# A squared-ReLU feed-forward computed by Strassen's seven block products

## The reference, cut to what matters

```python
x = x + mixed @ w_out[l]
h = _rms_norm(x, norm_mlp_g[l])
x = x + jnp.square(jax.nn.relu(h @ w_up[l])) @ w_down[l]
return _rms_norm(x, norm_final_g)
```

## Time and profile before

| | |
|---|---|
| median of 3 runs | 1752.92 us (1752.18 to 1753.65) |
| the profiled execution, its own time | 1755.03 us |
| its span, first to last instruction | 1752.9 us |
| TensorE clock granted, mean of the span | 0.986 |
| PE busy | 1672.7 us, 95% |
| DVE busy | 863.5 us, 49% |
| ACT busy | 683.2 us, 39% |
| POOL busy | 4.1 us |
| HBM read, written | 79.70 MB, 4.23 MB |

### The profile page before, as it was taken

How to read it: one execution, slowest core, us unless ns; L and a number is a source line. 1 busy time by engine, 2 the same in 40 slices (tenths; PEclk the granted TensorE clock), 3 DMA queues, 4 the chain that set the end, 5 groups by cost and what they waited for, 6 DMA issues and landing times.

```text
span 1752.9 us, 22515 instructions
## 1 busy us (share of the span) xinstructions
PE 1672.7 (95%) x8188; PEld 1373.6 (78%) x8188; DVE 863.5 (49%) x1738; ACT 683.2 (39%) x1484; POOL 4.1 (0%) x20
## 2 busy tenths in 40 slices
PE   6999898997999999999999999999999999999997
PEld 5777677774788887788888888888888888888886
DVE  5788888865566666422226344233333333323244
ACT  6467767773666666411114222121212121212121
POOL 0000000000000000000000000000000000000000
PEclk9999999997899999999999999999999999999998
DMA  5210100110020200112123302111111111111102
GB/s 180 78 33 25 37 25 25 37 37 0 13 61 14 60 13 22 34 43 57 42 71 106 109 25 72 49 48 48 48 48 48 48 48 48 48 48 48 36 12 96
DMA packets 126110, 84.95 MB, mean 48 GB/s; under 512 B 2888, under 2 KB 122696, under 8 KB 125904
## 3 DMA queue, kind: packets, MB, share of 16 engines
q1 hardware_dynamic: 126032, 83.94, 16.1%
HBM read 79.70 MB, written 4.23 MB: 48 GB/s over the span
## 4 chain that ended last, share of the span: by engine, by line
PE 78%; DVE 11%; issue 5%; ACT 5%; DMA 0%; ACTq 0%; DVEq 0%; SPq 0%
PE ps L525 36%; PE ps L829 20%; PE ps L569 11%; PE ps L638 3%; DVE work L1271 2%; PE ps L608 2%; PE ps L619 2%; DVE ps L1292 2%; PE ps L514 1%; ACT work L986 1%; DVE o_nat L1314 1%; ACT tmp L978 1%; DVE tmp L1256 1%; DVE work L1299 1%; DVE work L1263 1%
## 5 line engine op out<-in xcount | busy, mean ns | idle before, releaser
L569 PE MATMUL ps<-hspl,wsp 128*128 128x512 f32 x1536 | 427.6, 412 | 8.4 <-ACT tmp L942 6.6
L569 PEld LDWEIGHTS ps<-hspl,wsp 128*128 128x128 f32 x1536 | 268.9, 192 | 55.5 <-ACT tmp L942 8.6
L525 PE MATMUL ps<-hspl,wsp 128*128 128x512 f32 x1176 | 276.3, 392 | 0.6 <-ACT keep L1007 0.6
L525 PEld LDWEIGHTS ps<-hspl,wsp 128*128 128x128 f32 x1176 | 222.4, 189 | 47.1 <-issue 0.8
L829 PE MATMUL ps<-hspl,wsp 128*128 128x512 f32 x768 | 177.4, 390 | 0.0
L829 PE MATMUL ps<-hspl,work 128*128 128x512 f32 x768 | 175.4, 389 | 0.0
L1501 DVE TENSOR_TENSOR keep<-keep,ps 128x1024 f32<-128x1024 f32 x64 | 78.2, 1221 | 193.5 <-PE ps L829 192.5
L829 PEld LDWEIGHTS ps<-hspl,wsp 128*128 128x128 f32 x768 | 143.5, 188 | 32.6 <-DVE keep L1501 2.6
L829 PEld LDWEIGHTS ps<-hspl,work 128*128 128x128 f32 x768 | 144.2, 188 | 29.9
L525 PE MATMUL ps<-work,wsp 128*128 128x512 f32 x648 | 153.5, 390 | 0.0
L525 PEld LDWEIGHTS ps<-work,wsp 128*128 128x128 f32 x648 | 121.7, 188 | 25.7 <-issue 0.5
(11 more groups left out here) (158 smaller groups left out, 1738.9 us busy)
## 6 DMA issues: line engine op xcount, KB each, us to landing
raw<-in_w_in SPq DMA_DIRECT2D x47, 512.0 KB, 3.8
raw<-in_w_up SPq DMA_DIRECT2D x16, 512.0 KB, 4.0
tmp<-in_w_up SPq DMA_DIRECT2D x16, 512.0 KB, 4.0
raw<-in_w_down SPq DMA_DIRECT2D x16, 512.0 KB, 3.4
tmp<-in_w_down SPq DMA_DIRECT2D x16, 512.0 KB, 3.3
keep<-in_x SPq DMA_DIRECT2D x8, 512.0 KB, 6.6
fbias<-f_rows SPq DMA_DIRECT2D x8, 512.0 KB, 4.8
tmp<-in_x SPq DMA_DIRECT2D x8, 512.0 KB, 4.3
```

The lines of the kernel that those rows point to most:

```text
L525: ins = pe.matmul(ps[:, cols], w(wp, k), mv(mp, k)[:, cols], start=(k == 0 and n == 0), stop=(k == ks - 1 and n == 2))
L569: ins = pe.matmul(psp(u, g), wsp[:, c % 2, wp, k * P:(k + 1) * P], hspl[:, mp, k, cols], start=(n == 0), stop=(n == 23), skip_group_check= ...
```

## The change

The two feed-forward products are computed by the scheme of Strassen in Winograd's form. A product of two 2x2 block matrices takes 7 block products in place of 8, and in exchange sums of blocks before and after: with blocks a of the weights, blocks b of the activations, S1 = a21+a22, S2 = S1-a11, S3 = a11-a21, S4 = a12-S2, and likewise T1 to T4 of b.

Up and down become two stages. The up stage has 16 steps q, each a pair of 128 hidden columns; the blocks split the input channels and the tokens in halves. Each of its 7 products has 4 tiles x 3 = 12 matmuls. The down stage has 32 steps, 8 groups of hidden columns by 4 pairs of output channels, with 7 products of 2 tiles x 3 = 6 matmuls. The program is written out, without a loop.

The hidden values are stored in the DRAM tensor `hidden` as the seven forms that the down stage multiplies (`store_t`, `store_u11`, `store_u21`, `store_u22`), and loaded again (`load_b`). `kp` holds other values in the up stage, so the residual is stored in `x_mid` and loaded back (`reload`).

POOL forms the sums of weight blocks (`sums`, four 128-partition sums per step, 512 columns wide in the up stage and 256 in the down stage), of `h` (`h_sums`), of hidden values (`hidden_sums`, four sums 512 wide per up step), and adds three copied partial results to `kp` in the down stage (`add_s1`, `add_s2`, `add_s3`, 512 wide). ACT casts each of the seven forms (`form_hi`), DVE subtracts (`form_lo`). Partial sums stay in PSUM: ACT copies the bank (`copy_s1`, `copy_s2`, `copy_s3`) before the next product adds to it.

The output projection now goes over the two slots of `wsp` and in the order 0, 4, 1, 5, ..., and the forms of `h` are made beside it. After the down stage the sum of squares is kept by halves of the tokens.

The diff below is cut: declarations, the `t` and `u` stores that repeat a pattern, and the final stage's squares are left out.

```diff
+def block_products(n):
+    order = ((n, 0), (n - 1, 4), (n, 1), (n, 2), (n - 1, 5), (n, 3), (n - 1, 6))
...
+def block_forms(n):
+    order = [(n, j) for j in (4, 5, 6)] + [(n + 1, j) for j in (0, 1, 2, 3)]
...
+            def load_b(c, j):
+                if c < 2:
+                    sp.wait_ge(done, PRODUCT[UP - 1, j])
+                else:
+                    sp.wait_ge(done, PRODUCT[UP + 4 * (c - 2) + 3, j])
...
+                if n == UP - 1:
+                    load_b(0, 0)
+                    load_b(0, 1)
+                    load_b(0, 2)
+                    sp.wait_ge(a_lo, FORM[UP - 2, 5])
+                    reload(0)
+                    load_a_all(UP)
+                if n < UP:
+                    store_u11(n)
+                if n == UP - 1:
+                    sp.wait_ge(a_lo, FORM[UP - 2, 6])
+                    sp.wait_ge(a_sum, 4 * (UP - 1) + 3)
+                    reload(1)
+                    load_b(0, 3)
+                if 1 <= n < UP:
+                    store_u21(n - 1)
+                if n == UP:
+                    sp.wait_ge(a_lo, FORM[UP - 1, 6])
+                    reload(2)
+                    sp.wait_ge(t_ok, 4 * (UP - 1))
+                    sp.wait_ge(u11_out[0], 16 * (UP // 2))
+                    sp.wait_ge(u22_out[0], 16 * (UP // 2))
+                    reload(3)
+                    load_b(0, 4)
+                    load_a11(UP + 1)
+                    load_a12(UP + 1)
+                    load_a21(UP + 1)
+                    load_b(0, 5)
+                    load_a22(UP + 1)
+                    store_u21(UP - 1)
+                    load_b(0, 6)
+                    load_a_all(UP + 2)
...
+            def sums(q, ops):
+                pool.wait_ge(a_in[q % 4], 64 * (q // 4 + 1))
+                a = {x: a_raw_at(q, x) for x in FORM_RAW + ("a21",)}
+                for i in ops:
+                    if i == 1:
+                        if q >= 2:
+                            pool.wait_ge(done, PRODUCT[previous(q), 3])
...
+            def hidden_sums(q):
+                pool.tensor_tensor(t3b, u22[q % 2], u12, ALU.subtract).then_inc(t_ok, 1)
+                pool.tensor_tensor(t2b, t3b, u11[q % 2], ALU.add).then_inc(t_ok, 1)
+                pool.tensor_tensor(u12, u12, u11[q % 2], ALU.subtract).then_inc(t_ok, 1)
+                pool.tensor_tensor(t4b, u21, t2b, ALU.subtract).then_inc(t_ok, 1)
...
+            def add_s3(q):
+                c = down_c(q)["22"]
+                pool.wait_ge(s3_ok, q + 1)
+                pool.wait_ge(c22_ok, q + 1)
+                pool.tensor_tensor(c, c, s3[:], ALU.add).then_inc(add3, 1)
...
+            for n in range(1, NQ + 1):
+                if n >= 2 and n - 2 < UP:
+                    hidden_sums(n - 2)
+                if UP <= n < NQ:
+                    add_s1(n)
+                if UP <= n - 1:
+                    add_s3(n - 1)
+                if n + 1 < NQ:
+                    sums(n + 1, (1, 2, 3, 4))
+                if UP <= n < NQ:
+                    add_s2(n)
...
-            def mlp_block(b, first):
-                for j in range(4):
-                    if first:
-                        if j < 2:
-                            pe.wait_ge(resid, KC - 1 + j)
-                        else:
-                            pe.wait_ge(u_r, j - 1 + PRIME)
...
+            def product(q, j):
+                pe.wait_ge(a_lo, FORM[q, j])
+                if j == 0:
+                    if q < 3:
+                        pe.wait_ge(resid, 7 if q < 2 else 8)
+                        pe.wait_ge(c21_ok, q - 2)
+                elif j == 1:
+                    if q < 2:
+                        pe.wait_ge(xres, KC)
+                    else:
+                        pe.wait_ge(c11_ok, q - 1)
+                elif j == 2:
+                    pe.wait_ge(s1_ok, q + 1)
+                elif j == 3:
+                    if q == 0:
+                        pe.wait_ge(resid, KC)
+                    elif q < 3:
+                        pe.wait_ge(mean_out, 1)
+                    else:
+                        pe.wait_ge(c12_ok, q - 2)
+                elif j == 4:
+                    pe.wait_ge(s2_ok, q + 1)
+                elif j == 5:
+                    pe.wait_ge(s3_ok, q + 1)
+                else:
+                    pe.wait_ge(c22_ok, q + 1)
+                if q >= UP and (q - UP) % 4 == 0:
+                    pe.wait_ge(b_lo, HID_FORM[(q - UP) // 4, j])
+                o = bank_b(q) if j == 1 else bank_c(q) if j in (3, 6) else bank_a(q)
+                ks = 4 if q < UP else 2
+                for k in range(ks):
+                    if q == 0:
+                        h_form_ready(j, k)
+                    for m, (wp, mp) in enumerate(((0, 0), (0, 1), (1, 0))):
+                        w = (a_lo_at if wp else a_hi_at)(q, j)[:, k * P:(k + 1) * P]
+                        ins = pe.matmul(o, w, b_at(q, j, mp, k), start=(j in (0, 1, 3) and k == 0 and m == 0),
+                                        stop=(k == ks - 1 and m == 2), skip_group_check=True)
+                ins.then_inc(done, 1)
+            for n in range(NQ + 1):
+                for q, j in block_products(n):
+                    product(q, j)
+                    if (q, j) == (0, 1):
...
+            h_hi("t2", 3)
+            copy_s1(0)
+            h_hi("t13", 0)
+            h_hi("t13", 1)
             act.wait_ge(mean_done, 1)
             act.wait_ge(acc_ok, KC + 1)
             act.activation(tmp[:, 1, :], PS[2][:], ACT.Sqrt, bias=eps_c[:]).then_inc(mean_out, 1)
...
+            def down_block(n):
+                c, pair = divmod(n - UP, 4)
+                forms = next_forms(c, pair)
+                if n < UP + 2:
+                    form_hi(n, 4)
+                    square_hidden(u12, r12_ok, n - 1, u12_ok)
+                copy_s1(n)
+                if n >= UP + 2:
+                    form_hi(n, 4)
+                form_hi(n, 5)
+                copy_s3(n - 1)
+                form_hi(n, 6)
+                if n == UP:
+                    square_hidden(u22[(n - 1) % 2], r22_ok, n, u22_ok)
+                for x, j in forms[:1]:
+                    hidden_hi(x, j)
+                copy_s2(n)
+                if n + 1 < NQ:
+                    form_hi(n + 1, 0)
+                    form_hi(n + 1, 1)
+                for x, j in forms[1:]:
+                    hidden_hi(x, j)
+                if n == UP:
+                    square_hidden(u21, c21_ok, n, u21_ok)
+                if n + 1 < NQ:
+                    form_hi(n + 1, 2)
+                    form_hi(n + 1, 3)
...
+            def form_lo(q, j):
+                dve.wait_ge(a_hi, FORM[q, j])
+                dve.wait_ge(a_sum, 4 * q + (3, 4, 4, 2, 3, 1, 4)[j])
+                dve.tensor_tensor(a_lo_at(q, j), a_raw_at(q, FORM_RAW[j]), a_hi_at(q, j).bitcast(F32),
+                                  ALU.subtract).then_inc(a_lo, 1)
...
+            def down_add(q, what, read, source, signal):
+                c = down_c(q)[what]
+                dve.wait_ge(done, PRODUCT[q, read])
+                if what == "11":
+                    dve.wait_ge(add1, q - UP + 1)
+                elif what == "12":
+                    dve.wait_ge(add2, q - UP + 1)
+                elif q < UP + 4:
+                    dve.wait_ge(x_back[q - UP], 32)
+                elif what == "22":
+                    dve.wait_ge(add3, q - UP - 3)
+                dve.tensor_tensor(c, c, source, ALU.add).then_inc(signal, 1)
...
+            h_lo("t2", 3)
+            h_lo("t13", 0)
+            h_lo("t13", 1)
+            h_lo("t13", 2)
+            h_lo("t13", 3)
+            def up_block(n):
+                if n >= 2:
+                    up_c12(n - 2)
+                if n < UP:
+                    form_lo(n, 4)
+                if n == 0:
+                    for k in range(4):
+                        h_lo("t4b", k)
+                if n >= 2:
+                    up_r12(n - 2)
+                if n < UP:
+                    form_lo(n, 5)
+                if 0 < n <= UP:
+                    up_c22(n - 1)
+                if n < UP:
+                    form_lo(n, 6)
+                if 0 < n <= UP:
+                    up_r22(n - 1)
+                if n < UP:
+                    up_c11(n)
+                    form_lo(n + 1, 0)
+                    up_r11(n)
+                    form_lo(n + 1, 1)
+                if 0 < n <= UP:
+                    up_c21(n - 1)
+                if n < UP:
+                    form_lo(n + 1, 2)
+                    form_lo(n + 1, 3)
...
+            def down_block(n):
+                c, pair = divmod(n - UP, 4)
+                forms = next_forms(c, pair)
+                if n in (UP, UP + 1):
+                    up_c12(n - 2)
+                form_lo(n, 4)
+                if n in (UP, UP + 1):
+                    up_r12(n - 2)
+                form_lo(n, 5)
+                if n == UP:
+                    up_c22(n - 1)
```

(81 more changed lines are left out.)

788 lines of the change are left out of this document (590 added, 198 removed).

## The result

| | before | after |
|---|---|---|
| median of 4 runs | 1753.29 us | 1767.48 us |
| lowest, highest | 1752.18, 1754.13 us | 1765.99, 1768.46 us |

The ratio is 1.0079, 95% interval 1.0067 to 1.0091. The forecast was 1706 us, with 1672 to 1752 as its range: the change was expected to gain 47 us and costs 14. The profiled execution took 1765.99 us, its span is 1764.2 us, 11.3 us more than before.

The account below looks back on a forecast made before the run. PE was taken as the bound, without gaps in the feed-forward part. From the profiled 1755.0: -87.4 products, +18 down steps, +15 start, +3.5 clock, +8 change of stages, -4 end = 1708; against the median 1706 us, range 1672 to 1752.

Parts of the forecast that it names:

- Products removed, -87.4: Up and down products: 384 matmuls fall away at 0.2276 us each, -87.4 us.
- rival 4: Matmul groups: a quarter of 0.45 us extra in each of 336 groups, +37, 1743 us; chance 0.05.
- Start, +15 and +3.5: Start of up stage: PE stalls from DVE's queue behind the reciprocal, +15 us (10 to 20); lower clock afterwards, +3.5 (0 to 7).
- The up step: Steady up stage: 19.1 us a step at PE's pace, DVE and POOL work 16.4 us in turn, no loss.
- the like loop has 6 us spare: nothing: Up step: the loop resembling the down stage's through POOL and DVE has 6 us slack, so no cost.
- the down step's loop: Down step: PE, ACT, POOL sums and a DVE remainder take 7.4 us of 9.56, leaving 2.1 us spare.
- Change of stages, +8 with 2 to 20: Up to down: loads wait for last up products; first down step 3 us late, next two some 2 each; +8 us.
- Down step, 10.1 us with 9.56 to 11.4: Down stage: POOL and DVE hindering each other stretch 9.56 us steps to 10.1, +18 us in all (0 to +59).
- The end, -4: Kernel's end: half the tokens are summed and transposed while the other half is finished, -4 us (-8 to +3).
- Rival 2: Down step: slower POOL sums (1.5 us for 512) in turn with DVE, 13.0 us a step, 1798 us; chance 0.13.
- the down term: Down stage: +0.55 us in each of 32 steps from POOL and DVE hindering each other, +18 us (0 to +59).

Follow-up runs that it names:

- experiment 1: Changed kernel with POOL's two-input block sums replaced by constant writes of about the same length, reading nothing: 1713.25 us, 0.9763 of the kernel before.
- experiment 5: Changed kernel with DVE's reciprocal of the root replaced by a constant write: 1762.26 us, 1.0055 of the kernel before, 5.2 us less than the changed kernel.
- Experiment 3: Changed kernel with POOL making the next up step's first two sums ahead of the sums of hidden rows: 1751.95 us, 0.9987 of the kernel before.
- Experiment 4: Changed kernel with SP's first down-stage loads ahead of the stores waiting for POOL, and the first casts earlier: 1751.37 us, 0.9986 of the kernel before.
- experiment 6: Changed kernel with the down stage's third shared sum added by DVE from PSUM, not by ACT's copy and POOL: 1760.94 us, 1.0038 of the kernel before.

## Why the prediction was wrong, step by step

- **Products removed, -87.4: right.** The matmul did not get longer: the two windows of experiment 1 in which PE has no gap give 277.5/1222 = 0.2271 and 255.0/1127 = 0.2263 us, against 0.2276. So rival 4 is refuted.
- **Start, +15 and +3.5: right** in place and, nearly, in size (18.3, and 1.8 of clock behind P0(1)), with the mechanism shown by experiment 5. The two gaps are 13.0 us where 15.0 were forecast; three small waits (1.25, 0.48 and 0.26 us) that were not forecast make up the rest, and that is luck.
- **The up step, "the like loop has 6 us spare: nothing": failed**, +13.6 us, 11.9 of it in the loop. I had taken the down step's loop over to the up step, without working out the 6 us. But there POOL's four sums of hidden rows (1.3 to 1.8 us each) stand in program order between step n-2's squares and the sums of step n+1. The loop closes over them: POOL's `hidden_sums` 6.6 us, three sums 4.0, the stretched remainder, `r11`, casts, `c12`, `r12`, the square, and again `hidden_sums`: 20.44 us, although no engine but PE has over 60% to do. I had summed the work and not walked the order. Experiment 3 shows it.
- **Change of stages, +8 with 2 to 20: failed**, the largest error: 45.5 us. I had `load_b` wait for products, and overlooked that SP's `store_t` stands ahead of it and waits for POOL: a wait at nothing in the sum. By the products alone the loads could go behind P2(15), at 1348.2; the weights' were issued at 1355.0. They were there 8.2 us later, where I had 4, and the first hidden form's cast stood behind theirs on ACT. So P0(16) came 16.5 us late, not 3. Experiment 4 gives 16 of the 45.5 back; how the rest divides between the later loads, the stretched DVE work and the lower clock was not separated.
- **Down step, 10.1 us with 9.56 to 11.4: the hindrance right, its size and its path off.** It was 10.6 ((284.54 - 19.63) us over 25 steps), +26.4 over 27 steps instead of 15. The Trainium skill (SBUF — State Buffer, section "Who interferes with whom") says that a VectorE instruction with two SBUF inputs contends with a GpSimd one that reads SBUF, and not with one that only writes. Experiment 1 agrees: the two-SBUF-input operations go back from 0.840 to 0.423 us once POOL only writes, and those with a PSUM input stay (0.675 and 0.682). If all of this work had run in turn, 11.4 us would have come out; that much was not lost: 10.6 is a little over half the way from 9.56, where I took about a third. POOL's lengths were nearly right: 1.29 and 0.72 us undisturbed, for 1.19 and 0.68 assumed. By its loop I expected PE to wait at P0 for a remainder that waits for POOL. PE does wait there, but DVE hardly waits, 3 of 319 us: its own queue is full. And in a steady step (from 1510.48 us) the loop's five POOL operations took 1.31, 1.34, 0.92, 0.74 and 0.98 us, none of them 0.4 us over the 1.2 and 0.7 assumed; by my loop PE would not have waited.
- **The end, -4: near**, -2.5 us.

Rival 2 forecast the sign, but for another reason (13.0 us a step, and slower only from 11.6). Half of its condition was met: POOL's 512 is over 1.25 us, but DVE is not shut out for all of it, and the down step cost a quarter of what it said. From the 1708 us of the sum to the profiled execution's 1766 are 58 us: 49 are the two failed steps, 11 the down term, and the other terms, with the scatter before P0(0), take off 2.

## What to carry to other kernels

A sum of each engine's work does not bound a step: walk each engine's program order around the loop, and price whatever unrelated work stands between two of its operations. Where loads share a queue with stores, ask for each load what the store before it waits for, above all at a change of stages. Work given to POOL took from DVE where both read two SBUF operands (experiment 1), so what can take an operand from PSUM may be cheaper on DVE than it looks (experiment 6).

## What I had not expected of the hardware

- In the steady down steps, operations of DVE with two SBUF inputs took up to 3.7 times their length (0.41 to 1.52 us for 256 columns) beside POOL's, and POOL's up to 2.4 times (0.72 to 1.71); POOL's constant writes to SBUF, 66% of the time in the down stage, did not touch DVE (0.423 us).
- Moving an operation of 0.68 us to a DVE that was busy 99% of the time made its step 0.3 us shorter.
